# One bit of a threshold search in every unit, and its four selections moved into an up part

## The reference

```python
score = jnp.where(causal[None], score, -jnp.inf)          # 128 queries of a block x 1024 keys
_, idx = lax.top_k(score, topk)                           # topk = 256
...
att = jnp.where(valid[:, :, None, :], att, -jnp.inf)
p = jax.nn.softmax(att, axis=-1)                          # over the selected keys only

def channel_mixer(x, g_norm, w1, w2):                     # D_MODEL 1024, hidden 4096
    h = rms_norm(x, g_norm)
    return x + jnp.square(jax.nn.relu(h @ w1)) @ w2
```

## Time and profile before

| what | value |
|---|---|
| median of three runs | 2132.42 us |
| the profiled execution, its own time | 2130.93 us |
| its span | 2129.2 us |
| granted TensorE clock in it | 0.998 |
| TensorE busy | 98% of the span |
| VectorE, ScalarE, GpSimd busy | 63%, 47%, 48% |
| the stage in question | 344 to 700 us of the span |

### The profile page before, as it was taken

The page is one execution under the profiler, slowest core; times in us unless marked ns, Lnnn a source line. Parts: engine busy times, 40 slices in busy tenths (PEclk is TensorE's granted clock), DMA queues, the critical chain, the costliest instruction groups (busy, mean ns, idle before and its releaser), DMA issues.

```text
span 2129.2 us, 29538 instructions
## 1 busy us (share of the span) xinstructions
PE 2088.3 (98%) x9850; PEld 1742.6 (82%) x9850; DVE 1335.6 (63%) x2197; ACT 993.0 (47%) x1498; POOL 1019.4 (48%) x634
## 2 busy tenths in 40 slices
PE   7999899999999999999999999999999999999999
PEld 6888677888878898888888888888878888888887
DVE  7697657545481345268777645879853321779877
ACT  6554565665623564333323245435354323464552
POOL 6865753654646003556556556859774655000000
PEclk9999999999999999999999999999999999999999
DMA  5321112333323012223333232334323423433433
GB/s 215 99 64 57 70 38 62 109 99 99 99 70 109 21 53 80 89 80 111 97 99 100 89 92 90 106 89 139 99 89 99 135 93 113 144 119 109 139 128 119
DMA packets 69313, 208.30 MB, mean 98 GB/s; under 512 B 6976, under 2 KB 7232, under 8 KB 68928
## 3 DMA queue, kind: packets, MB, share of 16 engines
q1 hardware_dynamic: 69040, 206.57, 30.4%
q10 hardware_dynamic: 144, 0.02, 0.0%
HBM read 200.28 MB, written 6.29 MB: 97 GB/s over the span
## 4 chain that ended last, share of the span: by engine, by line
PE 87%; DVE 4%; issue 2%; ACT 1%; POOL 1%; DMA 0%; DVEq 0%; ACTq 0%; POOLq 0%; SPq 0%
PE psum L879 22%; PE psum L881 22%; PE psum L880 22%; PE psum L1225 5%; PE psum L1223 5%; PE psum L1224 5%; PE psum L1056 3%; PE psum L903 2%; PE psum L1032 1%; PE psum L1033 1%; POOL w_buf L1249 1%; PE psum L961 1%; PE psum L971 0%; PE psum L886 0%; DVE psum L2239 0%
## 5 line engine op out<-in xcount | busy, mean ns | idle before, releaser
L1249 POOL TENSOR_TENSOR w_buf<-raw,w_buf 128x1024 fp32r<-128x1024 f32 x270 | 659.4, 2444 | 488.4 <-ACT w_buf L1579 477.5
L879 PE MATMUL psum<-hid_buf,w_buf 128*128 128x512 f32 x1088 | 425.8, 391 | 0.0
L881 PE MATMUL psum<-hid_buf,w_buf 128*128 128x512 f32 x1088 | 423.7, 389 | 0.0
L880 PE MATMUL psum<-hid_buf,w_buf 128*128 128x512 f32 x1088 | 423.6, 389 | 0.0
L1579 ACT ACTIVATE w_buf<-raw 128x1024 fp32r<-128x1024 f32 x256 | 269.6, 1054 | 269.2 <-PE psum L881 216.0
L879 PE MATMUL psum<-h_buf,w_buf 128*128 128x512 f32 x960 | 376.7, 392 | 5.8 <-DVE xt L2411 4.1
L881 PE MATMUL psum<-h_buf,w_buf 128*128 128x512 f32 x960 | 373.7, 389 | 0.0
L880 PE MATMUL psum<-h_buf,w_buf 128*128 128x512 f32 x960 | 373.6, 389 | 0.0
L2434 DVE SCALAR_TENSOR_TENSOR psum<-y_buf,wdw,psum 128x512 f32<-128x512 f32 x435 | 294.9, 748 | 0.0
L880 PEld LDWEIGHTS psum<-hid_buf,w_buf 128*128 128x128 f32 x1088 | 204.4, 188 | 42.8 <-issue 0.7
L881 PEld LDWEIGHTS psum<-hid_buf,w_buf 128*128 128x128 f32 x1088 | 204.2, 188 | 42.9
(11 more groups left out here) (350 smaller groups left out, 3194.9 us busy)
## 6 DMA issues: line engine op xcount, KB each, us to landing
raw<-weights SPq DMA_DIRECT2D x320, 512.0 KB, 3.5
w_more<-weights SPq DMA_DIRECT2D x36, 512.0 KB, 3.9
xt<-x_t SPq DMA_DIRECT2D x2, 2048.0 KB, 8.2
out_t<-xt SPq DMA_DIRECT2D x16, 256.0 KB, 2.0
x_in<-x_t SPq DMA_DIRECT2D x12, 256.0 KB, 6.9
early<-weights SPq DMA_DIRECT2D x4, 512.0 KB, 7.6
x_kept<-xt SPq DMA_DIRECT2D x1, 2048.0 KB, 9.0
h_first<-x_kept SPq DMA_DIRECT2D x1, 2048.0 KB, 7.9
```

The costliest lines, as they stand in the source:

```text
L879: nc.tensor.matmul(acc, lhs_hi, rhs_hi, start=first, stop=False)
L880: nc.tensor.matmul(acc, lhs_hi, rhs_lo, start=False, stop=False)
L881: return nc.tensor.matmul(acc, lhs_lo, rhs_hi, start=False, stop=last)
L1249: nc.gpsimd.tensor_tensor(dst_lo, src, dst_hi.bitcast(F32), ALU.subtract).then_inc(done, 1)
```

## The change

Only the two tables change. Each of the units 1 to 31 takes one bit, units 32 and above none, and the four selections stand in units 33, 35, 37 and 39.

```diff
 KEY_UNITS = 48
-KEY_AT = [0] + [int(at % 4 > 0) for at in range(42)] + [0] * 5
-KEYS_DONE_AT = {43: 0, 44: 1, 45: 2, 46: 3}
+KEY_AT = [0] + [1] * KEY_BITS + [0] * 16
+KEYS_DONE_AT = {33: 0, 35: 1, 37: 2, 39: 3}
 assert sum(KEY_AT) == KEY_BITS
```

## The result

The changed kernel takes 2139.48 us (median of 8 runs), the kernel before in the same comparison 2132.39 us (8 runs): 7.1 us more, a ratio of 1.0035 with a 95% interval of 1.0024 to 1.0045. The forecast was 2138.1, +5.7 us. The profiled execution took 2140.32 us, with a span of 2138.6 us. Of all executions behind the medians of this text, one (of the one-input scan) ran at a granted clock of 0.655 and took 2994.94 us, and it is left out.

What follows compares the result with a forecast made beforehand. TensorE, busy for 98% of the span, was taken to bound the kernel, so only its standstills count. -5.3 + 1.1 + 9.9 = +5.7 us on 2132.4 gives 2138.1 us; own range 2136 to 2140.5, 8 in 10 2131.5 to 2141.5.

Steps and rivals of the forecast that it cites:

- What goes: TensorE's loss between units 48 and 52, around the end of the old selections, goes whole: -5.3 us.
- Unit 8: ScalarE's late start delays hidden tile 7, so TensorE stalls in unit 8: +1.1 us, bounds 0 and +1.5.
- The selections in the up part: VectorE and GpSimd hold each other up, hidden tile 39 comes late, TensorE stalls at unit 40: +9.9 us, bounds 0 and some 15.
- two pieces of the stall: Unit 40's stall comes as waits of some 4 and 5 us before its steps 6 and 7.
- plain sum: Up-part selections without hold-ups: tile 39 done at 35.8 us from the read of unit 33, under 37.2; nothing lost.
- first rival: The scan takes no part in the exclusion, only L2244 and L2248 wait: stall 4.6, sum +0.4, 2132.8 us; chance 0.20.
- second rival: VectorE and GpSimd seldom meet, TensorE keeps 5.44 us a unit: sum -4.2, 2128.2 us; chance 0.11.
- third: GpSimd wins each meeting, VectorE waits for the whole burst, weights for units 40 and 41 late too: 2144 us; chance 0.10.

Runs made afterwards that it cites:

- one-input scan: Changed kernel with the second input of the scan L2239 a zero in PSUM, so it reads one SBUF tensor: 2134.96 us, ratio 1.0008 to the kernel before.
- unit 1 free: Changed kernel with the bits in units 2 to 32, so unit 1 has no bit: 2138.58 us, ratio 1.0026 to the kernel before.
- one-input selections: Kernel before, its tables kept, with selections reading one SBUF tensor each in L2239, L2244 and L2248: 2130.82 us, ratio 0.9991 to the kernel before.

## Why the prediction was right, and where it was not

**What goes** was put at 5.3 us; 5.43 went.

**Unit 8** was put at 1.1 us: 1.53. The copies for units 5 and 10 came at 370.45 and 392.84, in an execution whose stage starts 0.6 us later. Tile 7 was done at 397.6 against a need at 391.49 + 4.76 = 396.3: 1.3 us, since ScalarE's run was not quite without a pause (it stood still for 0.40 us until 390.10). The other 0.2 us are the start behind the tile and the slower first matmuls, which the term left out.

**The selections in the up part** were put at 9.9 us: 0.31 + 10.83 = 11.1. The mechanism held step by step. In time from the read of 33, the read of 34 was expected at 13.2 us and came at 12.9; that of 38 at 37.5, and came at 37.3; tile 39 at 47.1, and was done at 46.7 (581.35). L2239, L2244 and L2248 were expected to wait 1.0, 1.4 and 2.1 us. The scan of 768 scores took 2.86 against 1.75 us, L2244 1.53 against 0.22, L2248 3.13 against 0.95: 1.1, 1.3 and 2.2. The two pieces of the stall, "some 4 and 5 us", were 4.12 and 3.85. From the need at 37.2 to 46.7 it is 9.5 us; the two waits are 8.0 of it, and the rest lies at the start of unit 40 and in the three matmuls between the waits, which already ran at 1.2 GHz. One step of the plain sum was off without changing the result: it has tile 39 done at 35.8 with no hold-up, but unit 39 can't be read before unit 40 starts, so 32.65 + 2.3 + 1.3 = 36.3 is the earliest. And 7.5 to 12 us of stall are 2135.7 to 2140.2 us by the prediction's own sum, not 2136 to 2140.5.

**The term that was missing** is what follows such a stall. TensorE over two stretches, the first with the second wait and all matmuls at 1.2 GHz, the second behind them; "PEclk" is the granted clock:

```profile
core 0: us, PE busy (x) PEld busy (x) DVE busy (x) ACT busy (x) POOL busy (x), PEclk, DMA share, GB/s
575.00:586.00 11.00, 6.24 (x17) 4.49 (x18) 10.24 (x9) 3.12 (x4) 9.69 (x5) 0.57 0.26 68
586.00:600.00 14.00, 14.00 (x63) 11.58 (x62) 1.38 (x2) 2.12 (x2) 6.18 (x3) 1.00 0.35 100
```

TensorE ran at 1.2 GHz from the first matmul behind the first wait (575.90) until about 584.5, a matmul every 0.43 us instead of 0.227. The seven matmuls at 1.2 GHz behind the second wait make up the 11.1 - 9.5 = 1.6 us: they took 3.1 us (581.40 to 584.54) instead of 1.6. So the stall was 0.4 us under its forecast and the clock 1.6 us over: +1.2, with +0.4 in unit 8 and -0.1 for what went, the whole distance between +5.7 and +7.2.

**The rivals.** The scan's part was the open question, and the first rival, that it takes no part, fell: the scans took 1.1 us more than their length, and the scan alone without its second SBUF input takes away 4.1 us (table) to 5.2 us (medians), against 5.3 between forecast and first rival. The second rival, that the engines seldom meet, fell to nine waits of VectorE in three selections. The third, that GpSimd wins each meeting and VectorE waits for the whole burst, fell because the scan took its turn between tile and split and held the split (3.84 us), and because L2244 ended with that split (553.49 + 1.53 = 555.02, the split 551.17 + 3.84 = 555.01) while a tile and a split of the burst were still to come. L2248 was issued beside the last split (556.22 + 2.39 = 558.61) and ended at 559.43, with 0.95 us of work of its own. That the exclusion lasts for the whole instruction, as the Trainium skill says ("SBUF — State Buffer", "SBUF: two separate sides"), fits these rows but for the last 0.13 us (559.43 - 0.95 = 558.48) and, the other way, 0.2 us (the held split ends 2.18 us behind the scan's 552.83 and takes 2.40 alone).

## What to carry to other kernels

Filler work on an engine (here the search and its selections) should stand where a late result only keeps a buffer full, not where it releases a chain: the same four selections, two units apart, cost nothing between residual reads and 11 us between reads that feed ScalarE, GpSimd and then TensorE itself. One unit apart they cost 5.4 us between residual reads too. Ask what a blocked read sets free all at once, since a burst on another engine meets the next piece of filler. If two engines shut each other out, as VectorE and GpSimd did here when a VectorE operation read two SBUF tensors, the place of the second input is a scheduling decision: one input moved to PSUM was worth 4 to 5 us in the up part, three of them 10, and nothing measurable where the banks covered the hold-ups.

## What the runs showed that was not expected

A stall costs more than its length when the clock falls in it or behind it. It fell in both profiles of the changed kernel and with unit 1 free (waits of 4.1 and 3.9 us with three matmuls between them, and already down behind the first), with the one-input scan (1.4 and 2.6 us, three matmuls between, down behind the second), and in before with one-input selections (0.3 and 2.4 us, a unit between). The kernel with only the bits moved waited 1.7 and 2.4 us, like before, and its clock fell; before kept it in three profiles of three. From 628 to 638 us, the kernel with the bits moved, and before in its second profile (columns as above):

```profile
628.00:638.00 10.00, 7.62 (x28) 6.21 (x28) 4.26 (x7) 5.46 (x8) 5.38 (x4) 0.83 0.05 7
```

```profile
628.00:638.00 10.00, 7.35 (x32) 5.81 (x32) 4.76 (x7) 5.47 (x8) 5.36 (x4) 1.00 0.06 9
```

The granted clock was 0.83 in one and 1.00 in the other, at a cost of 1.0 us (6.43 against 5.43). What decides it stays open.
